# Delta-rule heads: modulation tiles turned in 32x32 blocks and summed by VectorE, and the partial sums of all heads added by one product at the end

## What is computed

```python
c_act = jax.nn.silu(c)                           # 1 x 1024
mod = c_act @ w_ada[l] + b_ada[l]                # 1024 x 6144
sh1, sc1, g1, sh2, sc2, g2 = jnp.split(mod, N_MOD, axis=-1)
h = modulate(rms_norm(x, norm1_w[l]), sh1, sc1)
mix = hybrid_mixer(h, ...)                       # eight delta-rule heads, short convolution, gates
x = x + g1[:, None, :] * mix
h = modulate(rms_norm(x, norm2_w[l]), sh2, sc2)
x = x + g2[:, None, :] * swiglu(h, w_ffn_in[l], w_ffn_out[l])
...
shf, scf = jnp.split(c_act @ w_ada_f + b_ada_f, 2, axis=-1)
```

## Time and profile before

| | |
|---|---|
| time, median of 3 | 2182.2 us (2179.73 to 2184.66) |
| the profiled execution | 2180.72 us, its span 2178.7 us |
| PE busy | 2119.1 us, 97% of the span |
| DVE busy | 1318.1 us, 60% |
| ACT busy | 858.2 us, 39% |
| POOL busy | 425.7 us, 20% |
| mean granted clock of PE | 0.99 |

### The profile page before, as it was taken

The page is one execution under the profiler, slowest core; times in us unless marked ns, Lnnn a source line. Parts: engine busy times, 40 slices in busy tenths (PEclk is TensorE's granted clock), DMA queues, the critical chain, the costliest instruction groups (busy, mean ns, idle before and its releaser), DMA issues.

```text
span 2178.7 us, 29829 instructions
## 1 busy us (share of the span) xinstructions
PE 2119.1 (97%) x10312; PEld 1735.8 (80%) x10312; DVE 1318.1 (60%) x1905; ACT 858.2 (39%) x1352; POOL 425.7 (20%) x328
## 2 busy tenths in 40 slices
PE   6999999999999999999999999999999999999998
PEld 4788888888788878888888888888777777888886
DVE  6877787777544453334557555643788867555431
ACT  3333333333232232222335454422666635545321
POOL 0555775556600300000110000011000000000021
PEclk8999999999999999999999999999999999999999
DMA  7344433344333323333332333233221122333332
GB/s 295 100 114 125 116 106 106 104 117 125 88 96 116 116 77 96 96 96 90 99 114 68 96 96 96 83 105 101 59 58 50 54 83 86 96 96 96 94 95 73
DMA packets 394815, 216.81 MB, mean 100 GB/s; under 512 B 7880, under 2 KB 391298, under 8 KB 393219
## 3 DMA queue, kind: packets, MB, share of 16 engines
q1 hardware_dynamic: 393939, 213.51, 33.2%
q0 software_dynamic: 288, 2.10, 0.3%
q10 hardware_dynamic: 528, 0.40, 0.1%
HBM read 211.79 MB, written 4.19 MB: 99 GB/s over the span
## 4 chain that ended last, share of the span: by engine, by line
PE 75%; DVE 9%; issue 7%; POOL 5%; ACT 2%; DMA 1%; SPq 1%; POOLq 0%; ACTq 0%; DVEq 0%
PE ps L2201 23%; PE ps L2203 23%; PE ps L2202 23%; POOL ada_w L724 3%; PE ps L2374 1%; DVE small L2083 1%; DVE a_sb L2116 1%; DVE w_lo L1308 1%; DMA ada<-w_ada 1%; POOL gd_dia L747 1%; PE ps L2228 1%; DVE a_t_lo L2092 1%; ACT at_swap L1199 1%; DVE prob L2111 1%; POOL ada_s L724 1%
## 5 line engine op out<-in xcount | busy, mean ns | idle before, releaser
L2201 PE MATMUL ps<-h_hi,w_hi 128*128 128x512 f32 x1896 | 770.9, 407 | 7.1 <-DVE h_lo L1372 5.5
L2203 PE MATMUL ps<-h_hi,w_lo 128*128 128x512 f32 x1896 | 743.7, 392 | 0.0
L2202 PE MATMUL ps<-h_lo,w_hi 128*128 128x512 f32 x1896 | 742.2, 391 | 0.0
L1308 DVE TENSOR_TENSOR w_lo<-raw,w_hi 128x1024 fp32r<-128x1024 f32 x331 | 427.1, 1291 | 354.0 <-ACT w_hi L807 353.6
L807 ACT ACTIVATE w_hi<-raw 128x1024 fp32r<-128x1024 f32 x336 | 355.6, 1059 | 630.0 <-PE ps L2203 582.2
L2201 PEld LDWEIGHTS ps<-h_hi,w_hi 128*128 128x128 f32 x1896 | 358.8, 189 | 80.3 <-issue 13.9
L2203 PEld LDWEIGHTS ps<-h_hi,w_lo 128*128 128x128 f32 x1896 | 357.9, 189 | 78.1
L2202 PEld LDWEIGHTS ps<-h_lo,w_hi 128*128 128x128 f32 x1896 | 359.3, 189 | 64.9
L2201 PE MATMUL ps<-act_hi,w_hi 128*128 128x512 f32 x528 | 206.0, 390 | 0.0
L2203 PE MATMUL ps<-act_hi,w_lo 128*128 128x512 f32 x528 | 205.5, 389 | 0.0
L2202 PE MATMUL ps<-act_lo,w_hi 128*128 128x512 f32 x528 | 205.4, 389 | 0.0
(11 more groups left out here) (383 smaller groups left out, 2608.7 us busy)
## 6 DMA issues: line engine op xcount, KB each, us to landing
raw<-ffn_w_up SPq DMA_DIRECT2D x88, 512.0 KB, 3.7
raw<-w_in SPq DMA_DIRECT2D x72, 512.0 KB, 3.7
raw<-w_ffn_in SPq DMA_DIRECT2D x44, 512.0 KB, 3.7
ada_w<-w_ada SPq DMA_DIRECT2D x32, 512.0 KB, 3.9
raw<-ffn_w_down SPq DMA_DIRECT2D x32, 512.0 KB, 4.0
raw<-diff_w_qkv SPq DMA_DIRECT2D x24, 512.0 KB, 3.7
ada<-w_ada SPq DMA_DIRECT2D x8, 1024.0 KB, 12.4
ada_w<-w_ada_f SPq DMA_DIRECT2D x16, 512.0 KB, 3.8
```

Source lines behind the costliest of these rows:

```text
L1308: nc.vector.tensor_tensor(w_lo[:, tile.slot], raw[:, tile.raw], w_hi[:, tile.slot].bitcast(F32), SUB)\
L2201: nc.tensor.matmul(dst, w_hi[:, tile.slot, k], hi, start=first, stop=False)
L2202: nc.tensor.matmul(dst, w_hi[:, tile.slot, k], lo, start=False, stop=False)
L2203: return nc.tensor.matmul(dst, w_lo[:, tile.slot, k], hi, start=False, stop=last)
```

## The change

PE's six turns of `ada_s` and their step are gone from each head. DVE now turns `ada_s` itself, in blocks of 32 x 32 (two operations into `x_t` and `u_t`, which are free there), and sums each block row over 32 elements into a kept tile `ada_part` of 128 x (8 heads x 24). The bias is no longer added in the head. After the last head, and after its tail of fillers, PE multiplies `ada_part` by `quad` (a 128 x 32 tile of stacked identities, made by DVE ahead of the heads), which adds the four quadrants' parts. DVE adds the bias with eight operations of 32 partitions, and then comes to the ten small operations and `sc_lo`. The quarter that filled the place ahead of the turns moves behind them (two quarters in the last head).

```diff
-PE_STEPS += ["ada_turns", "o_turn"]
-DVE_STEPS += ["o_mean", "ada_sum", "ada_f_sum", "ada", "ada_f", "o_scale", "g_col", "o_gate", "o_lo"]
+PE_STEPS += ["o_turn"]
+DVE_STEPS += ["o_mean", "ada_turn", "o_scale", "g_col", "ada_sum", "o_gate", "o_lo"]
...
-HEAD_FILL.update(y0=2, v_new0=2, o_turn=3)
-LAST_FILL = dict(HEAD_FILL, y1=2, y2=2, y3=2, y4=2, y5=2, v_new0=2, v_new1=2, v_new2=2, ada_turns=2)
+HEAD_FILL.update(y0=2, v_new0=2, o_turn=4)
+LAST_FILL = dict(HEAD_FILL, y1=2, y2=2, y3=2, y4=2, y5=2, v_new0=2, v_new1=2, v_new2=2)
...
-    return 4 if steps is DVE_STEPS else 1
+    return 5 if steps is DVE_STEPS else 1
...
+        ada_part = sb("ada_part", [P, H, 24], at=masks_at + 4 * P * WHOLE_LEVELS)
+        quad = sb("quad", [P, 32], at=masks_at + 4 * P * WHOLE_LEVELS + 4 * 24 * H)
...
-                pool.wait_ge(g_pe, step(PE_STEPS, "ada_turns", h))
+                pool.wait_ge(g_dve, step(DVE_STEPS, "ada_turn", h))
...
-                after_pe("ada_turns")
-                nc.vector.tensor_reduce(small[:, S_ADA:S_ADA + 4], chunks(bank(2)), AX_X, ADD).then_inc(g_dve, 1)
-                nc.vector.tensor_reduce(small[:, S_ADA + 4:S_ADA + 6], chunks(bank(4))[:, 0:2], AX_X, ADD).then_inc(g_dve, 1)
-                own("ada_sum")
-                nc.vector.tensor_tensor(mod[:, bass.ds(4 * h + 16, 4)], small[:, S_ADA:S_ADA + 4],
-                                        vec[:, bass.ds(4 * h + (V_BADA + 16), 4)], ADD).then_inc(g_dve, 1)
-                own("ada_f_sum")
-                nc.vector.tensor_tensor(mod[:, bass.ds(2 * h + 48, 2)], small[:, S_ADA + 4:S_ADA + 6],
-                                        vec[:, bass.ds(2 * h + V_BADAF, 2)], ADD).then_inc(g_dve, 1)
+                after_pe(f"o{NC - 1}")
+                dve.wait_ge(g_pool, step(POOL_STEPS, "ada", h))
+                nc.vector.transpose(gd["x_t"][:], ada_s[:, 0:4].rearrange("p j c -> p (j c)"))
+                nc.vector.transpose(gd["u_t"][:, 0:2 * P], ada_s[:, 4:6].rearrange("p j c -> p (j c)")).then_inc(g_dve, 1)
...
+                own("ada_turn")
+                nc.vector.tensor_reduce(dyn(ada_part, h)[:, 0:16], gd["x_t"][:].rearrange("p (b c) -> p b c", c=32), AX_X, ADD)
+                nc.vector.tensor_reduce(dyn(ada_part, h)[:, 16:24], gd["u_t"][:, 0:2 * P].rearrange("p (b c) -> p b c", c=32),
+                                        AX_X, ADD).then_inc(g_dve, 1)
...
+            nc.vector.tensor_reduce(quad[:], ident.rearrange("p (b j) -> p j b", j=32), AX_X, ADD).then_inc(ada_all, 1)
             with dve.Fori(0, H - 1) as h:
                 head(HEAD, h, h)
             head(LAST, 0, H - 1)
+            dve.wait_ge(ada_all, 2)
+            sums = ps[0:32, 4, 0:24 * H].rearrange("p (h j b) -> p h j b", h=H, j=6)
+            for q in range(NC):
+                for c, r, js in ((16, V_BADA + 16, slice(0, 4)), (48, V_BADAF, slice(4, 6))):
+                    n = H * (js.stop - js.start)
+                    out3, add3 = [v[quadrant(q), at0:at0 + n].rearrange("p (h j) -> p h j", h=H) for v, at0 in ((mod, c), (vec, r))]
+                    modulated = nc.vector.tensor_tensor(out3, sums[:, :, js, q], add3, ADD)
+            modulated.then_inc(ada_all, 1)
+            dve.wait_ge(ada_all, 3)
             dve.wait_ge(g_dve, heads(DVE_STEPS, H))
...
-                fill("ada_turns")
-
-                pe.wait_ge(g_pool, step(POOL_STEPS, "ada", h))
-                for j in range(6):
-                    t = turn(part(bank(2 if j < 4 else 4), j % 4), ada_s[:, j])
-                t.then_inc(g_pe, 1)
                 fill("o_turn")
...
+            pe.wait_ge(ada_all, 1)
+            pe.wait_ge(g_dve, step(DVE_STEPS, "ada_sum", H - 1))
+            nc.tensor.matmul(ps[0:32, 4, 0:24 * H], quad[:], ada_part[:].rearrange("p h b -> p (h b)"), start=True, stop=True)\
+              .then_inc(ada_all, 1)
             pe.wait_ge(sc_split, 2)
```

More of the change, by code:

```diff
@@ L197 @@
 LAST_FILL["tail"] = 8
-assert sum(HEAD_FILL.values()) == 32 and sum(LAST_FILL.values()) == 48 and LAST_FILL["o_turn"] in (1, 2, 3)
+assert sum(HEAD_FILL.values()) == 32 and sum(LAST_FILL.values()) == 48 and LAST_FILL["o_turn"] > 0
 ATT_PE = ["scores0", "scores1", "v_turn", "scores2", "scores3"] + [f"turn{_q}" for _q in range(NC)] + ["pv", "sums", "rows"]
@@ L476, in block_kernel @@
         ada_land = [sem("ada_land0"), sem("ada_land1")]
-        ada_own = sem("ada_own")
+        ada_own, ada_all = sem("ada_own"), sem("ada_all")
         sc_split, mixed, mix_hi, mix_lo = sem("sc_split"), sem("mixed"), sem("mix_hi"), sem("mix_lo")
```

## The result

The changed kernel takes 2184.65 us (median of 21 runs, 2180.82 to 2187.21), the kernel before 2181.82 us on the same chip (21 runs, 2179.53 to 2184.66). The ratio is 1.0014, with a 95% interval of 1.0008 to 1.0020. That is 3.1 us more (1.7 to 4.4), where 4.4 was forecast: slower by a little, and within 0.2%. The forecast of 2186.6 us with its range of 2182.8 to 2190.2 held. The profiled execution of the changed kernel took 2183.44 us, its span is 2181.4 us.

A forecast was written before the change was run, and what follows sets the result against it. It took PE to be bound in the heads by its own queue or the path through o_turn. Heads -5.2, quad +0.2, end +7.1 and clock +2.3 gave +4.4 on 2182.2: 2186.6 us, range 2182.8 to 2190.2.

The forecast's parts named there:

- The turns leave PE, 0.65 us a head: PE's queue in each head: without the six turns eight heads give 5.2 us back; the y3 wait of 0.43 stays.
- the first rival: Step y3 in the heads: PE's wait for gd_dia goes too, 3.0 us more back, 2183.6 us; 8 in 100.
- DVE's turns and sums are covered: DVE in each head: costs nothing while extra work stays under about 2 us; 1 us spare at the gate.
- Quad, 0.2 us: Ahead of the heads: one more small DVE operation where the first head's chain begins, 0.2 us lost (0 to 0.3).
- The end, 7.1 us: Where the heads end: sc_lo waits behind product and additions, so PE's gate stage starts 7.1 us later (6.7 to 7.8).
- The estimate of 1.04 us for the additions: DVE's eight additions at the end: four held at 0.17 us and four not at 0.09, 1.04 us in all.
- The clock, 2.3 us: Behind PE's new stop at the gate stage: the clock falls to half, 2.3 us lost (1.6 to 2.8).
- The sum: Whole kernel: -5.2 + 0.2 + 7.1 + 2.3 = +4.4 us, 2186.6 us.
- Nothing later takes it back: After the heads: PE runs the gate stage and the two after it from its own queue, so the loss stays.
- the prediction's own sign of being wrong: Wrong if the HEAD round shrank over 0.65 us or not, the gate-stage stop were under 6, or another stall moved over 1.
- The bounds: Whole kernel: the bounds of the terms added up were said to give +2.9 to +6.3 us.
- The chances: Whole kernel: slower 48, within 0.2% 47, faster 5 in 100; the forecast itself had 77.

The follow-up runs named there:

- the three kernels without the stop: Changed kernel with sc_lo ahead of the additions on DVE, with the product ahead of PE's tail, or with both: 0.9978, 0.9972, 0.9975 of the kernel before.
- dve_plus1: Changed kernel plus 1.09 us of unread sums on DVE ahead of the gate in each head: 2185.91 us, 1.0020 of the kernel before.
- dve_plus3: Changed kernel plus, in each head, unread DVE sums of 1.09 us ahead of the gate and 1.89 us ahead of the turns: 2192.59 us, ratio 1.0046.
- filled twins: Unread matmuls fill PE's stop: changed kernel 1.0007 against 1.0017 unfilled; kernel before with the stop added 1.0030 against 1.0041.
- the first group's miss: Changed kernel with 30 unread matmuls in PE's stop: 2183.4 us, ratio 1.0012, against 1.0014 for the changed kernel, measured in another group.
- the stop without additions: Kernel before plus an unread product behind the tail, which DVE's ten small operations wait for: 2190.26 us, ratio 1.0042; run again 2190.89 us, 1.0041.

## Why the prediction was right, point by point

- *The turns leave PE, 0.65 us a head.* Right: 0.64 a round by the trace, and 4.8 to 6.1 us for the whole in the three kernels without the stop, where 5.0 was forecast. The wait at y3 stayed at 3.0 us, so the first rival fell.
- *DVE's turns and sums are covered.* Right, and with more room than said. I put the limit at about 2 us of extra work in all. The change adds 1.1 and leaves 1.35 us of idle time in front of the gate (I said 1), so the limit is near 2.5; dve_plus1 stays under it and dve_plus3 does not.
- *Quad, 0.2 us.* This term had no effect that the traces show. Quad's instruction took 0.38 us, behind 2.3 us in which DVE was idle. From the restart at 77.82 and 77.72 to the first o_turn are 65.9 and 65.2 us (to 143.70 and 142.96), 0.65 less, which the missing turns account for. In the four traced executions without quad this stretch lasts 65.9 to 66.1 us and in the nine with it 65.2 to 65.4.
- *The end, 7.1 us.* Right at 7.2: the product's record is 0.51 us (0.5), the eight additions 1.09 (1.1), the ten small operations 1.15 to the start of `sc_lo` (1.2), `sc_lo` 4.42 (4.43), and from its end to the first matmul 0.33 (0.33). The estimate of 1.04 us for the additions, made by the Trainium skill, "VectorE: DVE Perf Modes", section "Two Vector instructions with no wait between them", is near the 1.09 of this trace, and the trace bears the rule out. The eight start at 624.89, 624.99, 625.16, 625.27, 625.43, 625.54, 625.71 and 625.82: 0.11 us after the one in front where both write the same 32 partitions, 0.17 us where they do not, which is when the record of the one in front (0.15 us) has ended. So three of the eight are held and not four, as the prediction has it: the first one's output starts in the same group as that of the split before it.
- *The clock, 2.3 us.* Right in the profiled pair (5.0 us at half, 2.3 lost), and 2.4 and 2.2 us by the filled twins (2.0, from 1.2 to 2.8, with the first group's miss). That it hit the size this well is in part luck: in single executions the time at half was 3.1 to 5.5 us, which is 1.5 to 2.6 us. By the Trainium skill, "TensorE: Matmul & The Clock Gate", section "HAM oscillation", half of the time at the low clock is lost; the trace's spacings of 0.43 and 0.23 us say 47%, a difference that no run here could resolve.
- *The sum.* +4.4 was forecast, 3.1 and 3.7 us were measured (1.0014 and 1.0017), and the traces show the +4.3 standing at 770 us of the span. The parts measured by themselves are -5.5 for the heads and +9.1 for the stop without additions (1.0042 and 1.0041, 9.1 us), to which the additions add 1.1: +4.7. Where the last microsecond between that and the measured whole goes is not settled; it is within the intervals. In the profiled pair the clock at later stalls took back 2.4 us and the wait near 1566 cost 1.05 more, and that the changed kernel differs from the other in either wasn't shown. "Nothing later takes it back" was too strong a sentence for a single execution. By the prediction's own sign of being wrong, another stall that moves by more than a microsecond, the pair would even count against it; but that wait differs as much among executions with the same heads. The bounds were added up wrongly too: -5.6 + 0 + 6.7 + 1.6 is +2.7 and not +2.9; the range's lower end does not hang on it.
- *The chances.* They had slower by more than 0.2% at 48 and within 0.2% at 47. The measurement fell into the second, so on this the forecast was no better than a coin.

What makes the change slower as a whole is one place in the order. With the product ahead of the tail it is 2175.0 us, 0.9972 of the kernel before (product_early).

## What to carry to other kernels

Work that is moved to the end of a stage ("add up everything once") gets a new place in three queues, and the price is set by what stands behind it there. Here a 0.5 us product and 1.1 us of additions held back a 4.4 us operation that had been covered by PE's tail with nothing to spare. So look at what is covered exactly, and put the new wait behind it or its cause ahead of the cover. And count the clock: a stop of 7 us cost PE some 2 us more after it had ended. To know how much more work an engine can take, read its idle time in the round that repeats, not as a mean over all rounds, and count the new operations from start to start, not by their records.

## What was not expected of the hardware

The same stall did not always end in the same way. Behind the stop at the end the clock was at half for another 3.1 to 5.5 us in six executions. Behind the stall of 2.53 us ahead of 769.25 it was at half for another 3.1 to 5.9 us in all thirteen, which is 1.5 to 2.8 us lost. Behind the stall of 1.10 us near 1160 it fell in eleven and held in two. So a stall need not be long: 1.10 us of idle time mostly cost the clock for 3.4 us, and 1.6 us of time. Executions of one kernel differ by up to 7 us (2177.49 to 2184.2 among 23 of the kernel before); these falls may well be a large part of it, which was not tested.
